# Mask additions as matmuls, stick-breaking's values and norm in pieces, and the delta rule's faded keys moved into the inverse

## What is computed

```python
# first block, top-k attention, 4 heads
s = einsum(qb, k_sel) * scale;  p = softmax(where(valid, s, neg));  o_b = p @ v_sel
# second block, sparse attention: selected blocks and window, 6 heads each, causal
o_n = gate * softmax(where(causal, q @ k.T, NEG)) @ v;   head_rmsnorm(o_n, nsa_norm)
# second block, stick-breaking, 4 heads
log_1m = where(strict, log_sigmoid(-z), 0)
log_stick = cumsum(log_1m, reverse=True) - log_1m
a = where(strict, exp(log_sigmoid(z) + log_stick), 0);   o_s = a @ v
# second block, gated delta rule, chunks of 64, 6 heads
lower = where(strict, (k * beta) @ k.T * decay, 0)
u, w = solve(I + lower, [v * beta, k * beta * exp(g)])
state = state * exp(g_last) + (k * exp(g_last - g)).T @ v_new
```

## Time and profile before

| | us |
|---|---|
| median of 3 runs (lowest to highest) | 3344.66 (3342.47 to 3351.53) |
| profiled execution, its own time | 3343.76 |
| its span | 3341.8 |
| PE busy | 3172.3 (95%) |
| DVE busy | 1839.2 (55%) |
| ACT busy | 1303.3 (39%) |
| POOL busy | 390.2 (12%) |

### The profile page before, as it was taken

One profiled execution on the slowest core, in us unless ns is written; L12 is line 12 of the kernel. 1 busy time (PEld: TensorE's weight loads), 2 busy tenths in 40 slices (PEclk: granted clock), 3 DMA queues, 4 the chain that ended last, 5 costly groups with the idle time before them and its releaser, 6 DMA issues. The chain is left out here.

```text
span 3341.8 us, 48972 instructions
## 1 busy us (share of the span) xinstructions
PE 3172.3 (95%) x19264; PEld 2667.0 (80%) x19264; DVE 1839.2 (55%) x3260; ACT 1303.3 (39%) x2690; POOL 390.2 (12%) x354
## 2 busy tenths in 40 slices
PE   8999999999999999979999999999899989999996
PEld 6877788877877888868877888888788868888885
DVE  4875443436864434247466457474475565474644
ACT  4454433334354424234363333233443643332324
POOL 1021000000030000003013302010003034010100
PEclk9999999999999999989899999999999899999998
DMA  4111222222202222132100123222232000232231
GB/s 167 54 51 39 89 96 94 88 78 82 71 1 76 101 88 101 38 123 96 51 1 2 40 76 98 96 101 86 73 104 76 1 1 15 82 103 93 92 103 39
DMA packets 37341, 239.54 MB, mean 72 GB/s; under 512 B 4464, under 2 KB 5232, under 8 KB 15088
## 3 DMA queue, kind: packets, MB, share of 16 engines
q1 hardware_dynamic: 36528, 234.21, 20.6%
q10 hardware_dynamic: 576, 2.10, 0.2%
HBM read 234.19 MB, written 2.10 MB: 71 GB/s over the span
## 5 line engine op out<-in xcount | busy, mean ns | idle before, releaser
L265 PE MATMUL ps<-b_hl,bff_whl 128*128 128x512 f32 x704 | 274.2, 389 | 3.1 <-DVE b_hl L665 3.1
L267 PE MATMUL ps<-b_hl,bff_whl 128*128 128x512 f32 x704 | 274.0, 389 | 0.0
L266 PE MATMUL ps<-b_hl,bff_whl 128*128 128x512 f32 x704 | 273.9, 389 | 0.0
L248 DVE SCALAR_TENSOR_TENSOR bff_whl<-ring,b_cols,bff_whl 128x512 fp32r<-128x512 f32 (+1 forms) x224 | 153.2, 745 | 197.3 <-ACT bff_whl L235 197.0
L245 DVE TENSOR_TENSOR aff_whl<-ring,aff_whl 128x512 fp32r<-128x512 f32 x160 | 99.9, 687 | 224.8 <-ACT aff_whl L233 224.8
L235 ACT ACTIVATE bff_whl<-ring,b_cols 128x512 fp32r<-128x512 f32 (+1 forms) x224 | 136.6, 681 | 176.4 <-PE ps L267 176.4
L266 PE MATMUL ps<-aff_whl,a_u 128*128 128x512 f32 x512 | 204.3, 399 | 0.0
L265 PE MATMUL ps<-a_hl,aff_whl 128*128 128x512 f32 x512 | 200.8, 392 | 3.1 <-DVE a_hl L665 3.1
L265 PE MATMUL ps<-aff_whl,a_u 128*128 128x512 f32 x512 | 201.8, 394 | 0.0
L267 PE MATMUL ps<-aff_whl,a_u 128*128 128x512 f32 x512 | 200.7, 392 | 0.0
L266 PE MATMUL ps<-a_hl,aff_whl 128*128 128x512 f32 x512 | 200.5, 392 | 0.0
(11 more groups left out here) (521 smaller groups left out, 7804.7 us busy)
## 6 DMA issues: line engine op xcount, KB each, us to landing
ring<-in_a_w_ff SPq DMA_DIRECT2D x64, 1024.0 KB, 4.8
ring<-in_b_w_up SPq DMA_DIRECT2D x32, 1024.0 KB, 5.0
ring<-in_a_w_in SPq DMA_DIRECT2D x16, 1024.0 KB, 5.4
ring<-in_b_w_down SPq DMA_DIRECT2D x16, 1024.0 KB, 4.8
ring<-in_b_w_in_att SPq DMA_DIRECT2D x12, 1024.0 KB, 4.9
ring<-in_b_w_up SPq DMA_DIRECT2D x16, 768.0 KB, 4.2
ring<-in_b_w_in_conv SPq DMA_DIRECT2D x12, 768.0 KB, 4.4
ring<-in_a_w_out SPq DMA_DIRECT2D x8, 1024.0 KB, 4.9
```

The lines of the kernel that those rows point to most:

```text
L248: self.c.nc.vector.scalar_tensor_tensor(out=self.part(j, 1, k), in0=src[:, k, :], scalar=g[:, row + k:row + k + 1], in1=self.part(j, 0, k) ...
L265: nc.tensor.matmul(bank, sh, mh, start=start, stop=False)
L266: nc.tensor.matmul(bank, sh, ml, start=False, stop=False)
L267: return nc.tensor.matmul(bank, sl, mh, start=False, stop=stop)
```

## The change

There are four parts.

1. Masks. In the top-k attention all four tiles take their mask by a matmul: tile 0 with a causal mask in fp32r that ACT casts in the stage before, tile 3 with its search mask, which the search now writes beside the others. In the sparse attention of the second block tiles 0 and 1 take the product too. DVE adds no mask in either.
2. Stick-breaking. A head's values are multiplied in three parts, in three iterations of the loop (token tiles 0 and 1; 2; 3), and DVE's copy of the result comes one iteration later. The neighbour's norm squares, sums and scales by token tile.
3. `transpose_tiles` can be told which jobs DVE copies. Before the delta rule these are 2, 5 and 8 now, and ACT has the other nine.
4. POOL makes `kel` and `kbe` by token tile inside the inverse, `kbe` as keys times (beta x exp(g)); ahead of it only that small product is made.

```diff
@@ transpose_tiles @@
+    by_dve = list(range(1, len(jobs), 2)) if by_dve is None else list(by_dve)
+    by_act = [i for i in range(len(jobs)) if i not in by_dve]
...
+            if len(jobs) >= 8:
+                wait_kept(len(jobs) - 8)
             c.stay_busy(pe, len(jobs) % 8, 8)
@@ IndexSearch.late @@
-            step(nc.vector.tensor_scalar(self.tile(t) if t == TT - 1 else self.mask(t), self.tile(t), TAKEN, MASKED,
-                                         ALU.not_equal, ALU.mult))
+            step(nc.vector.tensor_scalar(self.mask(t), self.tile(t), TAKEN, MASKED, ALU.not_equal, ALU.mult))
@@ delta_inverse, POOL @@
             pool.wait_ge(cleared, 1)
+            for i in range(TT):
+                fade_keys(pool, i)
             for h in range(H):
...
                                         ).then_inc(started, 1)
+                if h < TT:
+                    fade_keys(pool, TT + h)
@@ stick_breaking, PE @@
-                    u = i - 5
-                    if 0 <= u < U and units[u][1] == 0:
+                    for late, tiles in ((5, (0, 1)), (6, (2,)), (7, (3,))):
+                        u = i - late
+                        if not (0 <= u < U and units[u][1] == 0):
+                            continue
                         h = units[u][0]
-                        if h == SB_H - 1:
-                            c.stay_busy(pe, 0, 10)
-                        pe.wait_ge(weights, u + 1)
...
-                        for t in range(TT):
+                        if tiles[0] == 0:
+                            if h == SB_H - 1:
+                                c.stay_busy(pe, 0, 10)
+                            pe.wait_ge(weights, u + 1)
...
+                        for t in tiles:
@@ stick_breaking, DVE @@
-                    if i == 3:
-                        nc.vector.tensor_tensor(sq[:], xo, xo, ALU.mult).then_inc(squared, 1)
-                    if i == 5:
-                        dve.wait_ge(squared, 1)
-                        nc.vector.tensor_reduce(ssq[:], sq[:], AX.X, ALU.add).then_inc(summed, 1)
+                    if 2 <= i < 2 + TT:
+                        t = i - 2
+                        nc.vector.tensor_tensor(sq[:, t], xo[:, t], xo[:, t], ALU.mult).then_inc(squared, 1)
+                    if 4 <= i < 4 + TT:
+                        t = i - 4
+                        dve.wait_ge(squared, t + 1)
+                        nc.vector.tensor_reduce(ssq[:, t], sq[:, t], AX.X, ALU.add).then_inc(summed, 1)
...
-                    if i == 12:
+                    if 13 <= i < 13 + TT:
...
-                    if 0 <= i - 3 < U and units[i - 3][1] == 1 and units[i - 3][0] >= 1:
+                    if 0 <= i - 4 < U and units[i - 4][1] == 1 and units[i - 4][0] >= 1:
@@ first_block @@
-                search.masks = sb3r("masks", [P, SCORE_AT[TT - 1]])
+                search.masks, causalr = sb3r("masks", [P, SCORE_AT[TT]]), sb3r("causalr", [P, P])
...
+                    nc.scalar.copy(causalr[:], c.causal)
...
-                                        lambda t: (c.causal, None, None, search.tile(3))[t],
+                                        lambda t: None,
...
-                                        mask_products=lambda t: (identr[:], search.mask(t)) if t in (1, 2) else None)
+                                        mask_products=lambda t: (identr[:], search.mask(t) if t else causalr[:]))
@@ attentions @@
-                              lambda t: (mask_product[0][:], mask_product[1][:]) if t >= 2 else None)
+                              lambda t: (mask_product[0][:], mask_product[1][:]))
@@ gated_delta @@
         def faded(pool, made):
-            nc.gpsimd.tensor_tensor(as4(g["kel"]), k4, wide(g["el"]), ALU.mult)
-            pool.wait_ge(made, 1)
-            nc.gpsimd.tensor_tensor(as4(g["kbe"]), as4(g["kb"]), wide(g["eg"]), ALU.mult)
-        transpose_tiles(c, "deltaT", jobs, faded, None, scaled, wait_scaled)
+            nc.gpsimd.tensor_tensor(g["beg"], g["beta"], g["eg"], ALU.mult)
+
+        def fade_keys(pool, i):
+            dst, by, t = (("kel", "el"), ("kbe", "beg"))[i // TT] + (i % TT,)
+            nc.gpsimd.tensor_tensor(as4(g[dst])[:, t], k4[:, t],
+                                    g[by][:, t].unsqueeze(2).broadcast_to([P, GDN_H, HD]), ALU.mult)
+        transpose_tiles(c, "deltaT", jobs, faded, None, scaled, wait_scaled, (2, 5, 8))
```

More of the change, by code:

```diff
@@ L471, in _, with wait_kept @@
         def _(pe):
+            def wait_kept(i):
+                if i in by_dve:
+                    pe.wait_ge(dve_kept, by_dve.index(i) + 1)
+                else:
+                    pe.wait_ge(act_kept, by_act.index(i) + 1)
             for i, (src, m, dst, scale) in enumerate(jobs):
                 if i >= 8:
-                    if i % 2:
-                        pe.wait_ge(dve_kept, (i - 8) // 2 + 1)
-                    else:
-                        pe.wait_ge(act_kept, (i - 8) // 2 + 1)
+                    wait_kept(i - 8)
                 if wait_source is not None:
@@ L489, in _ @@
                 ins.then_inc(turned, 1)
-            last = len(jobs) - 8
-            if last >= 0 and last % 2:
-                pe.wait_ge(dve_kept, last // 2 + 1)
-            elif last >= 0:
-                pe.wait_ge(act_kept, last // 2 + 1)
+            if len(jobs) >= 8:
+                wait_kept(len(jobs) - 8)
             c.stay_busy(pe, len(jobs) % 8, 8)
@@ L2793, in scale, with delta_inverse @@
         self.nc.vector.tensor_tensor(self.src, self.src, self.ssq.unsqueeze(3).broadcast_to(self.shape), ALU.mult)
-def delta_inverse(c, name, g, kT, kbT, qT, LT, attnT, dec, X, XT, whole, Y, M, norm_of, z4, z_gain):
+def delta_inverse(c, name, g, kT, kbT, qT, LT, attnT, dec, X, XT, whole, Y, M, norm_of, z4, z_gain, fade_keys):
     nc = c.nc
@@ L3894, in gated_delta @@
                           lambda sems: HeadNorm(nc, out_s, rows["sb_norm"].unsqueeze(1), half, sq, ssq, sems), z4,
-                          rows["gdn_norm"].unsqueeze(1))
+                          rows["gdn_norm"].unsqueeze(1), fade_keys)
         vn = hT[:, 3:5, :].rearrange("p a s -> p (a s)")[:, 0:2 * W].rearrange("p (a n) -> p a n", a=2)
```

34 lines of the change are left out of this document (19 added, 15 removed).

## The result

The changed kernel takes **3312.46 us** (median of three runs, 3312.18 to 3314.49) against 3344.66 (3342.47 to 3351.53); the ratio is 0.9909, 95% interval 0.9886 to 0.9932. The forecast was 3321, range 3312 to 3333: right in sign, just inside the range, and 8.5 us too cautious. The profiled execution took 3314.49 us (span 3312.7) at a mean granted clock of 0.982, where the one of before had 0.978.

What follows compares the result with a forecast made beforehand. TensorE, busy 95% of the span, was taken as the bound, so other engines' work pays only where it waits. 3343.8 - 6.6 - 2.8 - 8.6 - 5.8 = 3320.0, against the median 3320.9, said as 3321 us; range 3312 to 3333.

Steps and rivals of the forecast that it cites:

- sparse attention, masks: Second block's attention: stall before PE's transposes goes, two mask products cost 0.12 to 0.24; 0.30 a head, 6.6 us.
- top-k attention, masks: First block's attention: mask products on PE replace DVE's addition and PE's stall; net 1.4 us a layer, 2.8 in all.
- stick-breaking, structure: Stick-breaking stage: norm in pieces, values in three parts and the stage's end together gain 3.3 us a layer.
- stick-breaking, clock: Layer 0 of stick-breaking: shorter waits keep part of PE's clock; half of 3.9 us taken, 2.0.
- transposes: Before the delta rule: POOL's two products leave, ACT gets nine of twelve evictions; 2.9 us a layer, 5.8.
- keys in the inverse: Inverse: eight POOL products of 128x384 fit POOL's gaps; cost 0, cover 0.5 us each.
- Part (a): Stick-breaking's norm: quarter pieces shorten what stands before the next mask and softplus; 2.0 us a layer.
- Parts (b) and (c): Stick-breaking: (b) value products split between three units, 1.2 us a layer; (c) the stage's end, 0.1 us.
- the first: Rival: the clock doesn't come back in stick-breaking, or falls elsewhere as later stages shift; 3326 us, chance 0.2.
- The second: Rival: another wait takes over in the attentions, masks on PE buy nothing; 3330, chance 0.08; pure loss 3336, 0.02.
- third: Rival: POOL's key products in the inverse collide with DVE, costing 7.9 us; 3329 us, chance 0.08.
- The fourth: Rival: slower, PE stays at 1.2 GHz through a PE-bound stage; over 3355 needs 34 us lost, chance 0.02.

Runs made afterwards that it cites:

- norm-only run: Kernel before with only the neighbour's norm of stick-breaking in quarter pieces, values and copy left where they were; one execution, 3336.41 us.
- stick-only executions: Kernel before with only the stick-breaking stage changed, ten executions; 7.3 us less by medians than the kernel before.
- filled kernel: Kernel before with eight clock-keeping transposes at each of two waits behind stick-breaking's norm; median 3335.91 us, ratio 0.9984.
- last kernel but one: Changed kernel without stick-breaking's ten clock-keeping transposes, and with two waits of the compressed attention filled by such transposes; median 3304.28 us, ratio 0.9890.

## Why the prediction was right, and what it mis-sized

Term by term, forecast and measured (us, both layers):

```
sparse attention, masks                6.6    5.5
top-k attention, masks                 2.8    3.3
stick-breaking, structure              6.6    5.8
stick-breaking, clock                  2.0    7.3   (in this pair of profiles)
transposes                             5.8    6.7
keys in the inverse                    0.0    0.0
sum                                   23.8   28.6
```

The forecast lay 8.5 us above the measured time. About 4.8 of them are the difference of these sums, 0.5 came from the rest of the program, and 3.1 are that the medians differ by 32.2 us and the two profiled executions by 29.1. Without the clock the terms come to 21.3 us for 21.8, with errors of both signs that cancel. The result lies only 0.5 us inside the range, less than executions of one kernel scatter by, so that it is inside is partly luck.

**Masks.** The mechanism stood as put: the stall before the transposes went, and the products cost about their slot (some 0.13 us for a sparse head's two, where 0.12 to 0.24 was put). The sparse attention's size was 0.6 high a layer, because "with 11 heads a layer, since the first one fills the pipeline" took the stall as there from the second head on; the first heads of before had none, and there the products only cost. The top-k attention's was low by 0.25 a layer.

**Stick-breaking, structure.** The total was near (2.9 a layer for 3.3), part (a)'s share was not. Part (a), the norm, was given 2.0 and alone brings 1.0: "more instructions cost DVE up to 1.5 us in all, ... hence hidden" failed, because DVE's 7.07 of 9.75 us is a share, and the pieces stand in the one place of a head where PE waits for DVE. Parts (b) and (c), given 1.3, bring 1.4 alone and 1.9 beside the norm; the half more is the wait of the norm-only run, which is not there once the values are split.

**Stick-breaking, clock.** This is the term that was mis-sized most, 7.3 us in the pair of profiles for 2.0. "That layer is 3.9 us longer than the other with the same work" took the other layer as undisturbed. It wasn't (0.96 over the stage), and no window of the whole stage was read; only a head at 1.00 and a stretch at 0.50. The clock's part was 5.6 and 1.7 us, of which half of 3.9 was taken. How much of the 7.3 is the change and how much the profile that before happened to have, one pair can't say: the ten stick-only executions put the clock's part at about 1.3 us, nearer to the forecast's 2.0. The rule cited there, that a throttled PE is the default and activity releases it (the Trainium skill, "TensorE: Matmul & The Clock Gate", part 1), gave the better number for layer 0 of this pair. The runs bear it out as a tendency (seven of ten stages against one of sixteen), and against it stand the filled kernel's layer 1 and the busy stretch in which the clock fell.

**Transposes.** 6.6 us to the next stage was forecast and 6.61 came. The gain was low by 0.4 a layer because the working took 6.6 for the end of the clock-keeping transposes, and they end at 1771.05, 6.31 after the start; the next stage begins 0.3 behind that, as it did behind VectorE's last eviction before (1791.07 and 1791.39). That the lock between GpSimd and DVE was the cause (the Trainium skill, "SBUF — State Buffer", section "SBUF: two separate sides") is borne out: with GpSimd's two products gone and the stage otherwise as it was, the scaling fell from 4.36 to 1.83 us.

**The inverse.** Cost 0, as forecast, by the start of the last addition, which is the same to 0.02 us; the stage's whole length scatters too much (by 2.1 us with the same code) to show it. The cover was there, a fade took 0.83 us where 0.99 was put, and 1.5 to 2.5 us of GpSimd's idle time were left ahead of the first additions.

**The rivals.** Of the first, the half with the clock falling elsewhere happened stage by stage, but in the sum over the rest of the program it cost nothing (0.5 us less), and the clock did come back in stick-breaking. The second and third didn't happen. The fourth, slower by a lost clock, needs 34 us; the worst stick-breaking stages seen are 8.5 us over the undisturbed one.

## What to carry to other kernels

Before a stage's gain is forecast from two layers with the same code, read the mean clock over each whole stage: only a layer at 1.00 is a base, and it is one only if a second such layer agrees (stick-breaking's did to 0.01 us, the inverse's differ by 2.1). Take a stage's gain from its first row to the next stage's, not from a steady unit times their number: the wait that an edit takes away may not be there in the first units. When executions scatter with the clock, compare kernels at equal clock or by stage, since pieces of 7 us vanish in 6 us of scatter. Work given to PE pays exactly what PE waited there, so the same edit may be worth a third of a microsecond a head, nothing, or less than nothing where the wait isn't there; and pieces of a split instruction are hidden only where no one waits for that engine, whatever its busy share.

## What the runs showed of the hardware

The clock of one program differs from execution to execution: before had a mean of 0.975 to 0.984 in 25 executions, and 26 us between fastest and slowest. One stage of unchanged code took 45.2 to 53.7 us.

Busy rows don't hold the clock by themselves. In the last kernel but one it fell while PE's rows, matmuls of 31 rows and 64 columns and transposes of 31 columns, followed each other without a gap; with four 128x128 transposes in each later group it held through all of them in both layers. What exactly is counted stays open. Nor does every wait lose it: heads with waits of 0.6 and 0.8 us passed at 1.00 in most profiles.

A VectorE product of 128x1536 with both operands in SBUF took 4.36 us beside a GpSimd product of that shape and 1.83 without it. GpSimd's products of 128x384 (0.83 us) and VectorE's instructions of 128x512 with one operand in PSUM (0.7 us) ran at the same time with neither longer.

The inverse took 73.91 and 76.05 us with the same code, both at clock 1.00, with VectorE, ScalarE and GpSimd as long busy in the one as in the other to 0.2 us; why is open.
